# The long convolution of one layer put wholly on TensorE by shifted copies, and one conditioning set moved to another projection

## The reference

```python
CONV_WIDTH_2, D_MODEL, SEQ = 31, 1024, 256

def causal_dwconv(x, w, b):
    width = w.shape[0]
    xp = jnp.pad(x, ((0, 0), (width - 1, 0), (0, 0)))
    y = lax.conv_general_dilated(xp, w[:, None, :].astype(x.dtype), window_strides=(1,), padding='VALID',
                                 dimension_numbers=('NWC', 'WIO', 'NWC'), feature_group_count=x.shape[-1])
    return y + b

def adaln(c, w, b):                      # six vectors of 1024 for each layer, from silu(c)
    m = jax.nn.silu(c) @ w + b
    return [t[:, None, :] for t in jnp.split(m, 6, axis=-1)]

def conformer_conv_module(h, w_pw1, b_pw1, dw_w, dw_b, ln_g, ln_b, w_pw2, b_pw2):
    u = jax.nn.glu(h @ w_pw1 + b_pw1, axis=-1)      # 1024 -> 2048 -> 1024
    u = causal_dwconv(u, dw_w, dw_b)                # 31 taps, each channel by itself
    u = jax.nn.silu(layer_norm(u, ln_g, ln_b))
    return u @ w_pw2 + b_pw2
```

## Time and profile before

| | |
|---|---|
| device time, median of 3 runs | 2506.34 us (2505.02 to 2508.89) |
| the profiled execution | 2506.61 us, its span 2504.8 us |
| TensorE busy | 2330.6 us (93%) |
| VectorE busy | 1947.6 us (78%) |
| ScalarE busy | 1447.1 us (58%) |
| mean granted TensorE clock | 0.971 |
| DMA queue of SyncE | 64016 packets, 460.44 MB |

### The profile page before, as it was taken

One profiled execution on the slowest core, in us unless ns is written; L12 is line 12 of the kernel. 1 busy time (PEld: TensorE's weight loads), 2 busy tenths in 40 slices (PEclk: granted clock), 3 DMA queues, 4 the chain that ended last, 5 costly groups with the idle time before them and its releaser, 6 DMA issues. The chain is left out here.

```text
span 2504.8 us, 45660 instructions
## 1 busy us (share of the span) xinstructions
PE 2330.6 (93%) x18410; PEld 2221.1 (89%) x18410; DVE 1947.6 (78%) x3438; ACT 1447.1 (58%) x2673; POOL 12.8 (1%) x20
## 2 busy tenths in 40 slices
PE   8899999989999998889998979999988999988998
PEld 7899999978999998779997979997787999866998
DVE  6578798766688976968888868896559889857885
ACT  7535565465365645657746667656454775534764
POOL 0000000000000000000000000000000000000000
PEclk9999999999999999999999989999998999989999
DMA  6215577723175786214585525573425457722552
GB/s 248 89 52 203 189 285 299 303 85 120 50 256 206 285 320 228 85 68 169 192 311 221 202 93 179 201 286 135 169 84 185 167 189 304 272 97 89 197 186 101
DMA packets 64226, 463.36 MB, mean 185 GB/s; under 512 B 7248, under 2 KB 7440, under 8 KB 8208
## 3 DMA queue, kind: packets, MB, share of 16 engines
q1 hardware_dynamic: 64016, 460.44, 49.6%
HBM read 459.37 MB, written 1.05 MB: 184 GB/s over the span
## 5 line engine op out<-in xcount | busy, mean ns | idle before, releaser
L761 PE MATMUL psum<-arena_rounded,upper_rounded 128*128 128x256 f32 (+1 forms) x4792 | 1355.9, 283 | 75.8 <-DVE ring_rounded L572 22.2
L762 PE MATMUL psum<-arena_rounded,upper_rounded 128*128 128x256 f32 (+1 forms) x4792 | 1342.7, 280 | 0.0
L763 PE MATMUL psum<-arena_rounded,ring_rounded 128*128 128x256 f32 (+1 forms) x4792 | 1342.5, 280 | 0.0
L572 DVE TENSOR_TENSOR ring_rounded<-ring,upper_rounded 128x1024 fp32r<-128x1024 f32 (+4 forms) x958 | 838.3, 897 | 246.4 <-ACT upper_rounded L563 242.9
L563 ACT ACTIVATE upper_rounded<-ring 128x1024 fp32r<-128x1024 f32 (+4 forms) x958 | 751.0, 795 | 479.2 <-PE psum L763 385.6
L761 PEld LDWEIGHTS psum<-arena_rounded,upper_rounded 128*128 128x128 f32 (+1 forms) x4792 | 912.3, 190 | 93.8 <-issue 56.6
L762 PEld LDWEIGHTS psum<-arena_rounded,upper_rounded 128*128 128x128 f32 (+1 forms) x4792 | 910.6, 190 | 0.9 <-issue 0.5
L763 PEld LDWEIGHTS psum<-arena_rounded,ring_rounded 128*128 128x128 f32 (+1 forms) x4792 | 910.5, 190 | 0.0
L587 DVE CUSTOM_DVE_ANT_0 ring<-ring,silu_c,cols 128x1024 f32<-128x1024 f32 x192 | 244.7, 1279 | 0.0
L2502 DVE SCALAR_TENSOR_TENSOR arena<-psum,cols,arena 128x255 f32<-128x255 f32 (+1 forms) x352 | 153.2, 477 | 57.3 <-ACT arena L2469 54.2
L2469 ACT ACTIVATE arena<-psum,cols 128x256 f32<-128x256 f32 x176 | 89.5, 561 | 70.8 <-PE psum L763 68.7
(11 more groups left out here) (517 smaller groups left out, 2545.4 us busy)
## 6 DMA issues: line engine op xcount, KB each, us to landing
ring<-stream_dram SPq DMA_DIRECT2D x434, 1024.0 KB, 4.9
const<-const_dram SPq DMA_DIRECT2D x1, 1540.0 KB, 14.8
x<-x_dram SPq DMA_DIRECT2D x1, 1024.0 KB, 4.8
out_dram<-x SPq DMA_DIRECT2D x4, 256.0 KB, 2.0
cols<-cols_dram SPq DMA_DIRECT2D x1, 974.0 KB, 11.5
silu_c<-c_dram SPq DMA_DIRECT2D x1, 512.0 KB, 15.7
const<-const_dram SPq DMA_DIRECT2D x1, 67.0 KB, 4.6
pos<-positions_dram SPq DMA_DIRECT2D x1, 64.0 KB, 6.0
```

The lines of the kernel that those rows point to most:

```text
L572: dve.tensor_tensor(self.chip.rounded(raw), raw, self.chip.whole(upper), ALU.subtract).then_inc(self.lower_ready, 1)
L761: pe.matmul(out, upper, x[0][:, b.k, :], start=(b.k == 0), stop=False)
L762: pe.matmul(out, upper, x[1][:, b.k, :], start=False, stop=False)
L763: ins = pe.matmul(out, lower, x[0][:, b.k, :], start=False, stop=(b.k == nk - 1))
```

## The change

The convolution is done on TensorE for all eight tiles, and in another form. The 128 channels of a tile are four groups of 32. For each group q, the 128 partitions of `shifted[m][:, q]` are filled with four copies of its 32 channels, copy n shifted by n tokens; one matmul with 128 x 32 weights then does four taps of 32 channels, and eight rounds do the 31 taps (the 32nd has a zero weight). The output of group q lies in PSUM partitions 32q to 32q+31. A tile takes 4 x 8 = 32 matmuls of 128 x 32 weights and 256 columns.

The copies are made by DMA: 16 transfers for each tile (4 groups x 4 shifts), each of 32 partitions x 284 floats (36 KB) from SBUF to SBUF, all on SyncE's queue. `project` gets a hook (`beside`) that puts them between the loads of the ring. VectorE builds the weights of a tile in one instruction of 128 x 1024 (`build`) from the taps, which the host now lays out in that form, and a 128 x 32 pattern of four identities; ScalarE makes no diagonals any more and takes all eight tiles out of PSUM. The taps of tile m are inserted ahead of step m + 3 of `pw1`; those of tiles 5, 6 and 7 come after it, with the sums for the mean between them.

One of the two conditioning sets of the first down projection is now carried by `pw1`.

```diff
-            g["pw1", i] = by_rounds([...], TOGETHER)
+            g["pw1", i] = with_sides(by_rounds([...], TOGETHER), sides(1))
...
         g["ffn_down", i] = with_sides(by_rounds(matrix("ffn_w_down_2", (i,), F2, tiles(0, KD))),
-                                      sides(2 if i + 1 < L2 else 0))
+                                      sides(min(i + 1, 2) if i + 1 < L2 else 0))
...
     @block.sync
     def _(sp):
-        w.refill(sp, chip.groups[name])
+        at = 0
+        for step in range(steps if beside else 0):
+            to = max(n for n, b in enumerate(chip.groups[name]) if not b.side and b.tile // per == step) + 1
+            w.refill(sp, chip.groups[name][at:to])
+            at = max(at, to)
+            beside(sp, step)
+        w.refill(sp, chip.groups[name][at:])
...
+    shifted = [chip.place(7 * SLOT + 2 * T + m * GROUPS_CC * reach, GROUPS_CC, reach) for m in range(KD)]
...
-                    if m == 7:
-                        take(0)
+                    if m > lag:
+                        take(m - lag - 1)
...
-                    for tile, n in pe_taps[made:diagonals_by[m]]:
-                        act.activation(diagonal(made), chip.con("ident"), ACT.Identity,
-                                       scale=tap(tile, n)).then_inc(diagonals_ready, 1)
...
+                def build(m):
+                    if m >= ahead:
+                        dve.wait_ge(conv_ready, m - ahead + 1)
+                    dve.tensor_tensor(diagonals[m % ahead],
+                                      chip.col("dw_w", m * n_blocks, n_blocks).unsqueeze(2).broadcast_to([P, n_blocks, QUAD]),
+                                      over(chip.con("quads"), n_blocks), ALU.mult).then_inc(diagonals_ready, 1)
...
+        def taps(pe, m):
+            pe.wait_ge(shifted_ready[m], 16 * n_transfers)
+            pe.wait_ge(diagonals_ready, m + 1)
+            if m >= 2:
+                pe.wait_ge(conv_taken, m - 1)
+            for r in range(ROUNDS_CC):
+                for q in range(GROUPS_CC):
+                    ins = pe.matmul(chip.psum[QUAD * q:QUAD * (q + 1), conv_bank(m) * BANK:conv_bank(m) * BANK + T],
+                                    diagonals[m % ahead][:, q * ROUNDS_CC + r, :],
+                                    shifted[m][:, q, GROUPS_CC * r:GROUPS_CC * r + T],
+                                    start=(r == 0), stop=(r == ROUNDS_CC - 1))
+            ins.then_inc(conv_ready, 1)
+
+        def shift(sp, m):
+            sp.wait_ge(glu_ready, m + 1)
+            for n in range(GROUPS_CC):
+                for q in range(GROUPS_CC):
+                    sp.dma_start(shifted[m][QUAD * n:QUAD * (n + 1), q, :],
+                                 u[QUAD * q:QUAD * (q + 1), m, n:n + reach]).then_inc(shifted_ready[m], 16)
...
+            taps(pe, KD - lag)
+            for k in range(KD - lag - 1):
+                add_to_mean(k)
+            taps(pe, KD - 2)
+            add_to_mean(KD - 4)
+            taps(pe, KD - 1)
+            for k in range(KD - lag, KD):
+                ins = add_to_mean(k)
...
-                inserts={10: lambda pe: taps(pe, 0, half), 12: lambda pe: taps(pe, half, TAPS_CC - half),
-                         14: lambda pe: taps(pe, TAPS_CC, half)})
+                inserts={2 * (m + lag): lambda pe, m=m: taps(pe, m) for m in range(KD - lag)})
```

More of the change, by code:

```diff
@@ L67 @@
 BANK = 512
+QUAD = 32
+GROUPS_CC, ROUNDS_CC = P // QUAD, -(-TAPS_CC // (P // QUAD))
 MAGIC = 12582912.0
@@ L2550, in conformer @@
     e = [chip.place(7 * SLOT + b * T, T) for b in range(2)]
[L2551 to L2560, removed]
+    shifted = [chip.place(7 * SLOT + 2 * T + m * GROUPS_CC * reach, GROUPS_CC, reach) for m in range(KD)]
+    n_blocks = GROUPS_CC * ROUNDS_CC
+    ahead = 2 * SLOT // (n_blocks * QUAD)
+    diagonals = [chip.place(SLOT + m * n_blocks * QUAD, n_blocks, QUAD) for m in range(ahead)]
+    conv_bank = lambda m: 6 + m % 2
+    lag = 3
     w = chip.weights
+    n_transfers = GROUPS_CC * GROUPS_CC
     with fused(chip) as st:
[L2564 to L2567, removed]
+        whole_ready, upper_ready, lower_ready, glu_ready, conv_ready, conv_taken, diagonals_ready, mean_ready, \
+            centred, squared, var_ready, root_ready, *shifted_ready = st.signals(
+                "whole_ready", "x_upper_ready", "x_lower_ready", "glu_ready", "conv_ready", "conv_taken",
+                "diagonals_ready", "mean_ready", "centred", "squared", "var_ready", "root_ready",
+                *(f"shifted_ready_{m}" for m in range(KD)))
         @st.block.scalar
@@ L2679, in statistics @@
+        def shift(sp, m):
[4 more added lines that the diff above has]
+                                 u[QUAD * q:QUAD * (q + 1), m, n:n + reach]).then_inc(shifted_ready[m], 16)
         def statistics(pe):
-            taps(pe, TAPS_CC + half, 2 * TAPS_CC - half)
             ones = chip.con("ones")
-            order = [m for pair in on_dve for m in pair] + list(on_pe)
@@ L2683, in statistics, with add_to_mean @@
-            for k, m in enumerate(order):
-                if m in on_pe:
-                    pe.wait_ge(conv_taken, on_pe.index(m) + 1)
-                else:
-                    pe.wait_ge(taps_done, TAPS_CC * (k // 2 * 2 + len(on_dve[k // 2])))
-                ins = pe.matmul(chip.bank(0, T), ones, conv[:, m, :], start=(k == 0), stop=(k == KD - 1))
+            def add_to_mean(k):
+                pe.wait_ge(conv_taken, k + 1)
+                return pe.matmul(chip.bank(0, T), ones, conv[:, k, :], start=(k == 0), stop=(k == KD - 1))
@@ L3803 @@
             cols[:, at] = np.concatenate([a[0:D_NOPE]] + [a[lo:hi] for lo, hi in turned(D_NOPE)])
+        elif rows == "shifted":
+            for r in range(TAPS_CC):
+                part = cols[QUAD * (r % GROUPS_CC):QUAD * (r % GROUPS_CC + 1), at + r // GROUPS_CC:at + n:ROUNDS_CC]
+                part[:] = a[r].reshape(-1, QUAD).T
         elif rows is None:
```

66 lines of the change are left out of this document (17 added, 49 removed).

## The result

The changed kernel takes **2548.94 us** (median of 4 runs, 2547.71 to 2549.81) against 2507.61 us for the kernel before on the same chip: ratio 1.0162, 95% interval [1.0144, 1.018]. It is slower by 41 us; the forecast was 2484 us, 22 us faster. The profiled execution took 2547.71 us, 41.1 us over that of before.

A forecast was written before the change was run, and what follows sets the result against it. VectorE was taken to bound the conv module, late with its taps. Squares 19.8 us earlier plus 2.5 us from the conditioning set made 22.3 us off 2506.61: 2484 us; own range 2479 to 2489, 8 in 10 2478 to 2499.

The forecast's parts named there:

- I take 0.42 us: Price of one SyncE issue of a shifted copy, ends 0.39 and 0.55 us; a batch of 16 takes 6.7 us.
- The queue rival: SyncE's queue becomes the bound at 0.55 us an issue, 8.8 us a batch: 2494 us; chance 0.22.
- slow packets: Rival: small packets cost as much as large ones, 0.62 us a transfer; gain gone at 0.63 us; chance 0.05.
- SyncE needs 6.7 us and up to two loads (0.8 us) for each tile, so it keeps up: During pw1, SyncE's issues fit beside 9.1 us for each pair of taps and step.
- TensorE waits there 4.9 us: After step 2 of pw1, TensorE waits from 994.3 us until tile 0's shifts land at 999.2 us.
- so the wait is covered, just: After pw1, TensorE is busy until 1056.2 us, tile 7's shifts land at 1056.3 us; squares begin at 1062.9 us.
- The taps: Tile's taps on TensorE: four groups work side by side, eight rounds of 0.44 us plus 0.1 us, 3.65 us.
- The two rivals with the groups taking turns: Only three groups overlap, 4.8 us a tile, 2492 us, chance 0.12; or none, 14.2 us, 2568 us, chance 0.03.
- The clock loss: TensorE's clock falls after its wait before the first tile's taps: 2 us put in (0 to 2.8).
- The shifts' landing: Time from a batch's last issue until its copies are in place: 2.0 us, from the 256 KB stores.
- The conditioning set: First down projection, one set less: 2.5 us gained, between 0 and 5.6 us.
- At nothing, since VectorE is idle for half of it: VectorE's 8 builds and 8 pieces in pw1, 20 us, cost nothing; all its work is some 44 of 80 us.

The follow-up runs named there:

- the kernel with four issues a tile: Changed kernel, arena at its old place, four transfers a tile, each copying the first 32 channels to all four groups (values wrong): 2489.98 us, ratio 0.9896.
- the kernel with the arena put back: Changed kernel with the arena again at byte 112448 of each partition, position indices behind it: 2516.87 us, ratio to before 1.0046.
- the kernel through DRAM: Changed kernel, arena at its old place, copies made by one write to DRAM and four reads back a tile: 2502.77 us, ratio to before 0.9964.

## Why the prediction was wrong

- **The step that failed in the conv module is "I take 0.42 us" for an issue of the shifts.** Measured: 0.66 us from one to the next (a batch of 16 in 10.66 us; the instruction itself 0.59 us). It is not the full queue that makes them long: in the kernel with four issues a tile, whose queue has pauses, four of them take 2.53 to 2.95 us, 0.63 us or more each. The price came from loads of the ring, transfers from DRAM; the trace of before has no transfer from SBUF to SBUF, and 0.55 us was taken as the upper end though nothing bounded it there. The queue rival had the right mechanism and too small a price. The text even named the point from which the gain is gone, 0.63 us, but hung it on slow packets with a chance of 0.05; the DMA engines' busy share of 0.53 where shifts alone are issued speaks against those, and the kernel with four issues excludes them: as many bytes, and the wait is gone. At 0.66 us the eight batches and the loads between them fill the queue from 1000.44 to 1090.94 us. The four-issue kernel shows it: its module is 15.7 us shorter than that of before, where the changed kernel's is 9.5 us longer.
- **"SyncE needs 6.7 us and up to two loads (0.8 us) for each tile, so it keeps up"** falls with that price: it needs 10.6 us and up to 1.05 us for the loads, up to 11.7 us against the 9.1 us of a step with its taps. So do "TensorE waits there 4.9 us" (7.81 us) and "so the wait is covered, just" (5.23 us before taps 7, the squares at 1100.52 in place of 1062.9 us).
- **The taps were right to the row.** 3.65 us a tile; measured 3.66 us at full clock. Four groups do overlap in float32. The two rivals with the groups taking turns fall. The clock loss was right for one wait: the first tile's taps took 6.11 us, 2.5 us over the 3.66, where 2 us was put in; the granted clock of that stretch is 0.74. But the queue makes TensorE wait seven times, and the taps of all eight tiles are busy for 38.3 us in place of 8 times 3.66 = 29.3 us.
- **The shifts' landing**: 2.0 us put in, 2.7 us measured (5.8 us in the kernel with bigger transfers). Of what lies between the 15.7 us of the four-issue kernel and the 19.8 us forecast, 2.0 us are waits of TensorE for ScalarE to take a tile's sums out, 0.34 us or more before four tiles, which the timeline left out; the rest was not taken apart.
- **The conditioning set** was put at 2.5 us. By the waits of one execution it brings 1.4 us in the down projection, and by the module's length in one execution each (116.6 and 115.7 us) it costs 0.9 us in the new module: a size, 2 us off. "At nothing, since VectorE is idle for half of it" holds for the new module; in the old one the module with the set is 7.1 us longer.
- **The larger miss is a term that the sum puts at nothing without a reason.** It took every product outside the module as unchanged. The columns and constants that the change adds moved the arena by 128 bytes, and so its place relative to the weights, and the 15,000 products follow each other 2.5 ns later on average: 38 us by the gaps' sum, some 30 us by the kernel with the arena put back. Why the place acts on the spacing stays open. No rival named it. The line that aligns the arena was in the code, and the trace of before had both spacings, x170 and x179 in stretches that are all "busy 20.00".
- **"What would show it"** had "batches over 9 us" for the queue: seen.

## What to carry over

Price a DMA issue by a row of the same direction and size, and where there is none, treat the queue's total (issues times price) as an open bound: it was the decisive number of this module. Before timing an edit that adds to a resident table, compare the addresses of everything allocated behind it; a kernel with padding alone tells the effect of a placement from that of the edit. Where TensorE is "busy" throughout, count its instructions in equal stretches before calling two of them alike.

## What was not expected of the hardware

- The spacing of 256-column products depends, in nine layouts of the kernel before, on where the arena with the moving operands lies relative to what stands ahead of it, the weights most likely, modulo 256 bytes: mean gaps of 114.1 to 115.2 ns at -64, 116.9 to 119.9 ns at the five other differences. The common gaps are 113 to 114 and 117 to 119 ns at -64 and +64, 120 ns at 0, and 115 to 123 ns at -128, -96 and -32.
- An issue from SBUF to SBUF into 32 partitions lasts 0.59 to 0.61 us (median) whether it moves 36, 71 or 142 KB; the reads of 142 KB from DRAM in the kernel through DRAM last 0.43 us.
- A write of one tile to DRAM took 7.4 us to landing in the running module, where the four stores at the end take 2.0 us.
